# Two transformer blocks on one core: the second block's key search, gated linear attention and attention put in another order

## The reference

```python
proj = h @ w_in                    # q,k,v; q_idx,k_idx,w_idx; gla q,k,v; gdown, ogate
# attention a (8 heads of 64): each query keeps its top-k keys
score = sum_h relu(q_idx . k_idx) * w_idx ; _, sel = top_k(score, 128)
p = softmax(q.k/8 + bias[bucket] over the kept keys) ; o_a = p @ v
# attention b: gated linear attention (4 heads, chunks of 64)
bcum = cumsum(log_sigmoid(gdown @ w_gate_up + b)/16)
q_in, k_in, k_dec = q*exp(bcum), k*exp(-bcum), k*exp(blast - bcum)
o_b = tril(q_in k_in^T) v + q_in state ; state = state*exp(blast) + k_dec^T v
o_b = rmsnorm(o_b) * silu(ogate)
x = x + concat(o_a, o_b) @ w_out ; then a gated FFN and a final norm
```

## Time and profile before

| | us |
|---|---|
| median of 3 runs (lowest, highest) | 2067.23 (2066.11, 2072.78) |
| the profiled execution's own time | 2067.12 |
| its span | 2065.1 |
| PE busy in the span | 1952.7 (95%) |
| DVE, ACT, POOL busy | 889.0, 716.0, 501.8 |

### The profile page before, as it was taken

How to read it: one execution, slowest core, us unless ns; L and a number is a source line. 1 busy time by engine, 2 the same in 40 slices (tenths; PEclk the granted TensorE clock), 3 DMA queues, 4 the chain that set the end, 5 groups by cost and what they waited for, 6 DMA issues and landing times.

```text
span 2065.1 us, 21914 instructions
## 1 busy us (share of the span) xinstructions
PE 1952.7 (95%) x8805; PEld 1523.8 (74%) x8805; DVE 889.0 (43%) x1486; ACT 716.0 (35%) x1032; POOL 501.8 (24%) x272
## 2 busy tenths in 40 slices
PE   7989889999999999999799999998997889999998
PEld 6766667887878777877588888865775678888886
DVE  6677766203041303343233334568435554433443
ACT  5545554232322322433122223423336432222223
POOL 4322224444444434410000000232235401100100
PEclk9999999999999999999899999998999989999999
DMA  9322324521213122325623322421121123232321
GB/s 304 126 82 86 102 78 133 184 87 62 96 62 102 61 82 96 108 82 82 113 82 102 102 86 66 119 62 61 62 69 54 42 72 102 82 102 87 97 92 51
DMA packets 183019, 192.22 MB, mean 93 GB/s; under 512 B 10690, under 2 KB 166632, under 8 KB 182792
## 3 DMA queue, kind: packets, MB, share of 16 engines
q1 hardware_dynamic: 179752, 180.84, 27.4%
q0 software_dynamic: 1744, 4.99, 2.1%
q10 hardware_dynamic: 1424, 5.00, 0.7%
HBM read 186.09 MB, written 4.72 MB: 92 GB/s over the span
## 4 chain that ended last, share of the span: by engine, by line
PE 81%; DVE 12%; DMA 3%; ACT 2%; issue 2%; POOL 0%; SPq 0%; DVEq 0%; ACTq 0%; POOLq 0%
PE bank L1401 21%; PE bank L1402 21%; PE bank L1404 20%; DMA stg<-in_w_ffn_in 2%; PE bank L1421 2%; PE bank L1423 2%; PE bank L1422 2%; PE bank L1506 2%; DVE tmp L1770 1%; DVE spl L1776 1%; DVE SW L2021 1%; DVE sph L1774 1%; DVE small L2019 1%; DVE tmp L1732 1%; PE bank L1462 1%
## 5 line engine op out<-in xcount | busy, mean ns | idle before, releaser
L2543 POOL TENSOR_TENSOR wl<-stg,wh 128x1024 fp32r<-128x1024 f32 x150 | 362.2, 2416 | 973.5 <-ACT wh L2201 973.4
L1401 PE MATMUL bank<-hH,wh 128*128 128x512 f32 x1296 | 543.2, 419 | 22.5 <-DVE wl L1714 14.5
L1402 PE MATMUL bank<-hL,wh 128*128 128x512 f32 x1296 | 521.6, 403 | 0.0
L1404 PE MATMUL bank<-hH,wl 128*128 128x512 f32 x1296 | 520.9, 402 | 0.0
L2201 ACT ACTIVATE wh<-stg 128x1024 fp32r<-128x1024 f32 (+2 forms) x292 | 298.1, 1023 | 327.1 <-PE bank L1404 220.7
L1401 PEld LDWEIGHTS bank<-hH,wh 128*128 128x128 f32 x1296 | 249.4, 192 | 106.5 <-issue 50.7
L1404 PEld LDWEIGHTS bank<-hH,wl 128*128 128x128 f32 x1296 | 249.3, 192 | 61.0
L1402 PEld LDWEIGHTS bank<-hL,wh 128*128 128x128 f32 x1296 | 250.2, 193 | 51.6 <-issue 0.7
L1714 DVE TENSOR_TENSOR wl<-stg,wh 128x1024 fp32r<-128x1024 f32 (+2 forms) x142 | 168.3, 1187 | 252.6 <-ACT wh L2201 252.1
L1401 PE MATMUL bank<-h2H,wh 128*128 128x512 f32 x352 | 141.4, 402 | 0.0
L1402 PE MATMUL bank<-h2L,wh 128*128 128x512 f32 x352 | 140.7, 400 | 0.0
(11 more groups left out here) (323 smaller groups left out, 2760.3 us busy)
## 6 DMA issues: line engine op xcount, KB each, us to landing
stg<-in_w_in SPq DMA_DIRECT2D x54, 1024.0 KB, 5.2
stg<-in_w_ffn_in SPq DMA_DIRECT2D x22, 1024.0 KB, 5.1
stg<-in_w_ada SPq DMA_DIRECT2D x16, 1024.0 KB, 5.3
stg<-in_w_ffn_gate SPq DMA_DIRECT2D x11, 1024.0 KB, 5.3
stg<-in_w_ffn_up SPq DMA_DIRECT2D x11, 1024.0 KB, 5.3
stg<-in_w_ffn_down SPq DMA_DIRECT2D x10, 1024.0 KB, 5.0
stg<-in_w_ada SPq DMA_DIRECT2D x16, 512.0 KB, 6.6
stg<-in_w_proj_ret SPq DMA_DIRECT2D x8, 1024.0 KB, 5.0
```

The source lines that it names most:

```text
L1401: T.matmul(ps, wh, xh, start=j["first"] and k == 0, stop=False)
L1402: T.matmul(ps, wh, xl, start=False, stop=False)
L1404: t = T.matmul(ps, wl, xh, start=False, stop=j["stop"] and last)
L2543: G.tensor_tensor(lo, src, hi, ALU.subtract).then_inc(s["w_lo_pool"], 1)
```

## The change

1. `select` yields twice after each pair of heads. The rate of GQ, GK, GV goes from 0.85 to 0.65.
2. The stage after them holds QA, the four gates, KA (rate 1.1), and VA comes where the gates were (0.97); the first half of w_out goes from 1.0 to 0.97.
3. The gates' products go to `LG` tiles, `gate_silu` follows a job later; `gn` is followed by the product with the gate on POOL.
4. `tm` moves to ACT as a plain copy; the norm is put on after the turn, in four 128-wide activations with `rt3` as scale. The turns take a G bank.
5. `gf`, `gh`, `gi` move from DVE to POOL.
6. `attn` is written anew: bias plus mask (`lg`) one item ahead, `al(n)`, `ae(n-1)`, yield, `at(n-2)`, `lg(n+1)`, `ac(n-2)`, `ag(n)`, yield, `av(n-3)`, `as(n-1)`, yield. `av` takes bank 7, and waits only for its own pair's part of VA.
7. The results of gla have tiles of their own (`goH`, `goL`, where GQ, GK, GV lay) and are split one per job from the attention's start on. `matn` is set at the start of the second block.

```diff
     def turn_after(name, e):
         def turn():
-            take("Z", ("tmt", name, e))
+            take("G", ("tmt", name, e))
...
                 if hh % 2:
                     yield
+                    yield
...
-    stage(0.85)
+    stage(0.65)
...
+                while ("silu", hd) not in p.known:
+                    yield
                 emit("gn", hd)
...
     for e in range(2):
+        fm(2872 + 256 * e, "gate", [(2 * e,), (2 * e + 1,)], after=silu_after)
+    for e in range(2):
         fm(512 + 256 * e, "fm", [("KA", 2 * e), ("KA", 2 * e + 1)])
-    for e in range(2):
-        fm(1024 + 256 * e, "tm", [("VA", 2 * e), ("VA", 2 * e + 1)], after=turn_after)
-    stage(0.9)
+    stage(1.1)
...
         for n in range(len(ITEMS) + 3):
-            for lag, step in ((2, lambda n: emit("as", n)), (1, greatest), (0, logits), (1, lambda n: emit("ae", n)), (3, last),
-                              (2, turned), (2, copied)):
+            if wanted(n, 0):
+                logits(n)
+            if wanted(n, 1):
+                emit("ae", n - 1)
+            yield
+            if wanted(n, 2):
+                turned(n - 2)
+            if n and wanted(n + 1, 0):
+                emit("lg", n + 1)
+            if wanted(n, 2):
+                emit("ac", n - 2)
...
+            if wanted(n, 0):
+                emit("ag", n)
...
+            yield
+            if wanted(n, 3):
+                while ("VA", ITEMS[n - 3][0]) not in p.known:
+                    yield
+                values(n - 3)
+            if wanted(n, 1):
+                emit("as", n - 1)
+            yield
...
     def start_attn():
-        emit("matn")
         p.fore.append(attn())
+        for hd in range(4):
+            p.later.append([hd, lambda hd=hd: split_go(hd)])
...
-    for k0, rate in ((4, 1.0), (0, 0)):
+    for k0, rate in ((4, 0.97), (0, 0)):
...
+            def tm(name, e, n):
+                gb = product(ac, n)
...
+                A_.activation(TMP[2 + e % 2][:, :], gb[:, :], ACTF.Copy).then_inc(empty(("gemm", n, 0)), 1)
...
+                for i in range(4):
+                    t = A_.activation(dst[:, i, :], zb[:, i * P:(i + 1) * P], ACTF.Copy, scale=rt3[:, i:i + 1])
...
+            def gf(r):
+                po.wait_ge("a_ge", r + 1)
+                emptied(po, of_job("fm", "GK", r))
+                G.tensor_tensor(TMP[4][:, :], TMP[4][:, :], GK[:, r, :], ALU.mult).then_inc(s["p_gf"], 1)
```

More of the change, by code:

```diff
@@ L757, in start2 @@
         emit("two_load")
+        emit("matn")
         p.fore.append(factors3())
@@ L776, in turn @@
         def turn():
-            take("Z", ("tmt", name, e))
+            take("G", ("tmt", name, e))
             emit("tmt", name, e)
             give(("tmt", name, e))
+            p.known.add((name, e))
         p.later.append([1, turn])
@@ L891, in make_plan, with silu_after, silu @@
     do(lambda: p.fore.insert(0, interleave(p.fore.pop(0), gla()) if p.fore else gla()))
+    def silu_after(hd):
+        def silu():
+            emit("gate_silu", hd)
+            p.known.add(("silu", hd))
+        p.later.append([1, silu])
     for e in range(2):
@@ L902, in attn, with wanted, logits, turned @@
     def attn():
-        def last(n):
+        def wanted(n, lag):
+            return 0 <= n - lag < len(ITEMS)
+        def logits(n):
+            pr, i = ITEMS[n]
+            if i == 0 and pr + 1 < 4:
+                for hh in range(2):
+                    emit("bias_row", 2 * pr + 2 + hh)
+            for hh in range(2):
+                take("Z", ("al", n, hh))
+            emit("al", n)
+        def turned(n):
+            for hh in range(2):
+                take("C", ("at", n, hh))
+            emit("at", n)
+        def values(n):
             pr, i = ITEMS[n]
             if i == 0:
-                take("G", ("avo", pr), 0)
+                take("O", ("avo", pr), 0)
             emit("av", n)
@@ L915, in last @@
                     pend.append(pr)
[L917 to L939, removed]
         for hh in range(2):
             emit("bias_row", hh)
+        emit("lg", 0)
+        emit("lg", 1)
         for n in range(len(ITEMS) + 3):
-            for lag, step in ((2, lambda n: emit("as", n)), (1, greatest), (0, logits), (1, lambda n: emit("ae", n)), (3, last),
-                              (2, turned), (2, copied)):
[L945 to L948, removed]
+            if wanted(n, 0):
[9 more added lines that the diff above has]
+                emit("ac", n - 2)
+                for hh in range(2):
+                    give(("at", n - 2, hh))
+            if wanted(n, 0):
+                emit("ag", n)
+                for hh in range(2):
+                    give(("al", n, hh))
+            yield
[6 more added lines that the diff above has]
+            yield
@@ L950, in start_attn, with split_go @@
+    def split_go(hd):
+        p.split("h4", 4 + hd, "dve")
+        emit("gos", hd)
     def start_attn():
-        emit("matn")
         p.fore.append(attn())
+        for hd in range(4):
+            p.later.append([hd, lambda hd=hd: split_go(hd)])
     do(start_attn)
     for e in range(2):
-        fm(2872 + 256 * e, "gate", [(2 * e,), (2 * e + 1,)])
-    stage(0.65)
-    def split_go():
+        fm(1024 + 256 * e, "tm", [("VA", 2 * e), ("VA", 2 * e + 1)], after=turn_after)
+    stage(0.97)
@@ L959, in split_go, with h_free @@
+    def h_free():
         p.known.add("h_free")
         p.mark("h4")
-        for hd in range(4):
-            p.split("h4", 4 + hd, "dve")
-            emit("gos", hd)
         for pr in pend:
@@ L966, in split_go @@
             emit("qas", pr)
-    do(split_go)
+    do(h_free)
     def out2_job(f2, k0):
@@ L1080, in program @@
         vw = [(cell(4), cell(4)) for _ in range(2)]
+        rt3 = cell(4)
         with ExitStack() as ph:
@@ L1141, in program @@
             tmp9 = sb("tmp9", [P, S], ctx=ph)
+            with ExitStack() as ph1:
+                GQ = sb("GQ", [P, 2, S], ctx=ph1)
+                GK = sb("GK", [P, 2, S], ctx=ph1)
+                GV = sb("GV", [P, 4, S], ctx=ph1)
+            with ExitStack() as ph1:
+                goH = sb("goH", [P, 4, S], F32R, ctx=ph1)
+                goL = sb("goL", [P, 4, S], F32R, ctx=ph1)
         with ExitStack() as ph:
@@ L1165, in operand @@
                 return orH[:, k, :], orL[:, k, :]
+            if what == "h4" and k >= 4:
+                return goH[:, k - 4, :], goL[:, k - 4, :]
             if what == "mg":
@@ L1652, in av @@
                 pr, i = ITEMS[n]
-                for e in range(4):
-                    emptied(pe, ("tmt", "VA", e))
+                emptied(pe, ("tmt", "VA", pr))
                 emptied(pe, ("at", n, 0))
@@ L1840, in sprd @@
                 ve.wait_ge("v_spread", 5 * i - 4)
+                if key == "n3":
+                    V.tensor_scalar(rt3, w, 1.0, None, ALU.mult).then_inc(s["v_extra"], 1)
                 for c in range(4):
@@ L2075, in gs @@
                 zb = filled(ve, ("gs", hd))
+                ve.wait_ge("p_gh", 2)
                 if hd:
@@ L2453, in gsq, with gate_silu @@
                 A_.activation(tmp8[:, :], TMP[5][:, :], ACTF.Square).then_inc(s["a_gsq"], 1)
[L2455 to L2458, removed]
+            def gate_silu(hd):
+                emptied(ac, of_job("gate", hd))
+                A_.activation(LG[hd][:, :], LG[hd][:, :], ACTF.Silu).then_inc(s["a_gate"], 1)
             def ae(n):
@@ L2601, in al @@
                     po.wait_ge(f"d_bias{bia % 4}", 16 * (bia // 4 + 1))
+                    if n < 2:
+                        po.wait_ge("p_gate", 2 * n + hh + 1)
                     if n >= 3:
@@ L2617, in gpsimd @@
             mine = {"split": split, "n1": n1, "masks": masks_, "sbw": sbw, "ret_load": ret_load, "rot": rot, "rvv": rvv,
-                    "bias": bias, "ffn_a": ffn_a, "gate": gate, "al": al, "qas": qas}
+                    "bias": bias, "ffn_a": ffn_a, "gf": gf, "gh": gh, "gi": gi, "gn": gn, "lg": lg, "qas": qas}
             for name, *at in p.order:
```

80 lines of the change are left out of this document (33 added, 47 removed).

## The result

The changed kernel takes 2035.64 us (median; 2032.27 to 2038.67), the kernel before 2067.88 in the same comparison: ratio 0.9845, 95% interval 0.9829 to 0.9861. Run again later it took 2037.85, ratio 0.9856 (0.9836 to 0.9876). The forecast was 2038.

A forecast was written before the change was run, and what follows sets the result against it. PE's waits, on VectorE's search queue in A and the list's order in B, plus half clock behind them, were taken as the bound. -9.4 and -19.4 make -28.8 on 2067.1: 2038, own range 2024 to 2050, wider 2020 to 2058.

The forecast's parts named there:

- A: Second block, end of MI job to end of VA, 184.0 us before: 18.7 lost in place of 26.9, -9.4 in all.
- B: Attention, from A's end to end of w_out's first half, 112.4 us before: 8 lost in place of 28.6, -19.4.
- 10.7 us of waits: PE's waits left in A: `gt` 3.3, `go` 2.4 and 3.4, another 1 for the rest, 0.6 in tile 3.
- The clock: Half-clock spells of 3.3 us behind PE's waits: two or three in A, 8 us; 3 us in B.
- the search's spread: `select` over 75 turns in place of 63: line 1576's waits (7.3) go but 0.6; DVE nearly full in the next 70 steps.
- the price of `gf` on POOL: POOL's products take 0.1 to 0.64 us longer; only `gf` precedes PE's next step, its cost counted in first `gt`'s 3.3 us.
- rival 3: POOL's six products in gla all stand behind a weight split: 18 us on gla's chain, 2056 us in all; chance 0.05.
- DVE is as good as full, and stalls move rather than vanish: In A's 70 steps after GV, DVE has 66 us of work against PE's 69.
- late hand-overs: In the attention's new loop, engines fit between yields with little to spare; occasional late hand-overs cost 3 us.
- The start: Attention's start: `lg(0)` may wait for bias rows that leave SP only after the weight split two blocks back: 2 us.
- v on ACT: Eight evictions leave DVE, ACT gains about 8.6 us, hidden by its idle time: cost 0, bounds 0 to 2.
- rival 2: B bound by DVE and POOL sharing their access; items stay long, B loses 20, 2051 us in all; chance 0.08.

The follow-up runs named there:

- the second profile: Profile of the changed kernel run again unaltered: A 179.1, B 90.0; median 2037.85 us, ratio 0.9856.
- the first gap: Changed kernel with two more yields between `gf` and the turn `gt`, rate 1.15 for 1.1: 2035.65 us, ratio 0.9848.
- the early bias: Changed kernel with more yields before `gt` and `go`, rate 1.2, plus first item's bias rows and `lg(0)` ahead of gla's last head: 2028.26 us, ratio 0.9803.
- the last version: Changed kernel with more yields before `gt` and `go`, first item's bias and `lg(0)` earlier, and v evicted by VectorE: 2023.96 us, ratio 0.9790.

## Why the prediction came out right, point by point

**The sum.** -9.4 for A and -19.4 for B were forecast, -28.8; measured -6.5 and -23.8, -30.3 (by the second profile -4.9 and -22.4). The total is right because the two errors, 2.9 us too much in A and 4.4 too little in B, have opposite signs; that they nearly cancel is luck. The executions' own spread is as large.

**A: the idle time is right, its places are not.** 10.7 us of waits were forecast; the window has 177.5 - 166.07 = 11.4. The clock kept 0.05 x 177.5 = 8.9, 8 forecast. The prediction put all of A's gain but 1.2 us down to the search's spread; it is needed, but alone it earned nothing. And `gt(0)` was to wait 3.3, `gt(1)` not at all and the two `go` 5.8; they waited 3.0, 4.3 and 2.5. The step that failed is the price of `gf` on POOL ("its price is in the 3.3"): it holds for the first pair only. Its input was misread too: the 1222 ns of VectorE's product "beside POOL's own work" is the mean of one of 0.69 and one of 1.75 us, and only the second met a weight split on POOL (from 1436.08 to 1438.42). DVE's timeline of the kernel before:

```profile
1437.21 1.75 DVE L2043 TENSOR_TENSOR tmp<-tmp,GK 128x512 f32<-128x512 f32 x1
```

The timelines of the changed kernel around the second turn:

```profile
1430.73 0.69 DVE L2058 TENSOR_TENSOR tmp<-tmp 128x512 f32<-128x512 f32 x1
...
1432.18 0.60 ACT L2431 ACTIVATE tmp<-bank 128x512 f32<-128x512 f32 x1 [0.74 <-DVE SW L2029]
1432.67 0.62 ACT L2455 ACTIVATE tmp<-tmp 128x512 f32<-128x512 f32 x1
1433.19 1.05 ACT L2208 ACTIVATE wh<-stg 128x1024 fp32r<-128x1024 f32 x1
...
1434.32 2.34 POOL L2563 TENSOR_TENSOR wl<-stg,wh 128x1024 fp32r<-128x1024 f32 x1 [5.76 <-ACT wh L2208]
1436.62 1.71 POOL L2614 TENSOR_TENSOR tmp<-tmp,GK 128x512 f32<-128x512 f32 x1
...
1438.38 1.11 PE L1466 MATMUL bank<-ident,tmp 128*128 128x128 f32 x4 [4.33 <-POOL tmp L2614]
```

VectorE is done at 1431.4. ACT's exp (2455) stands behind a relu that waits for a score; POOL's product (2614) stands behind a weight split (2563) that itself waits for ACT's high part, which lies behind that exp. Three queues in a row are each passed in their order, and 1.71 us of product end in a wait of 4.3. This is rival 3's mechanism, at one of its six places. On the same k-steps with VectorE's product, in the kernel with the spread alone, `gt` waited 3.6 and at most 0.8, and `go` 5.3: the prediction's waits were those of that kernel. What POOL cost at `gt` came back at `go`, which the prediction had not seen; part of that is how the engines happened to meet (last section).

**Stalls move.** "DVE is as good as full, and stalls move rather than vanish" was half true. DVE isn't full while PE waits for `gt(1)`; windows of 20 us of the changed kernel:

```profile
1400.00:1420.00 20.00, 16.98 (x70) 13.22 (x70) 19.05 (x44) 8.26 (x14) 9.21 (x5) 0.91 0.17 53
1420.00:1440.00 20.00, 14.84 (x56) 9.13 (x57) 13.54 (x15) 9.35 (x16) 8.02 (x5) 0.91 0.17 52
```

In the second PE idles 5.2 us and DVE 6.5. The stall there is latency through three queues. It moved all the same, three times: from `idx2` to `go` with the spread alone, from `gt` to `go` with VectorE's products and with the first gap. A fell clearly further only when both hand-overs were given distance, to 170.2, 171.9 and 167.9; 5.6 of the 9.8 us of waits were still there in the first of these.

**B: too careful.** 8 us were to stay lost; the window has 88.6 - 84.95 = 3.7 idle and clock 1.00 (in the second profile 3.6 and 0.98). The order acts as worked out, but late hand-overs were 2 us, not 3, and they drew almost no half clock. The term that was mis-sized is thus the clock: 3 us forecast, next to none measured. The start was priced right (2; 1.7) for a wrong reason. The changed kernel's timelines of SP and POOL:

```profile
1514.66 0.90 SPq L1361 DMA_DIRECT2D bia<-scratch_bias  x2
...
1524.55 0.86 POOL L2647 TENSOR_TENSOR lg<-bia,matn 128x128 f32<-128x128 f32 x2
```

The bias rows leave SP nine us ahead of `lg(0)`; what holds it is the gate's product and the weight split on POOL, as the early bias shows.

**v on ACT** was priced at 0, with 0 to 2 as bounds. Undone, B is 2.5 to 3.9 us shorter and A the same; undone in the last version, B is 1.4 shorter (88.3 to 86.9) and A 4.0 (171.9 to 167.9). No median tells it apart from nothing, but both point to a loss. The activations with `rt3` as scale:

```profile
L2423 ACT ACTIVATE GV<-bank,small 128x128 f32<-128x128 f32 x16 | 4.6, 378 | 1.2 <-PE bank L1466 1.2
...
1540.11 1.14 ACT L2423 ACTIVATE VA<-bank,small 128x128 f32<-128x128 f32 x4
```

Each took 0.37 to 0.38 us, not 0.27. But they overlap, and four in a row took 1.14 us, close to the 1.08 forecast, so their time is not what the prediction had wrong. The Trainium skill (ScalarE: Activation LUTs, section What ACT_TABLE_LOAD costs) gives about 93 ns for each pointer operand of an activation; the rows nearly agree, 378 against 269 ns. PE did wait for ACT's copies of v, once, 1.1 us; the prediction named that as a sign against it.

**The other signs.** Waits behind `ag` below 4 us: 1.7. Waits left on `gt` with POOL's product and on `go` with the mask product: yes. Clock 0.96 or more in both: B yes, A 0.95. A near 175 and B near 93: 177.5 and 88.6. No table loads among the exps: one is left in B, at its start, where before had nine.

## What to carry to other kernels

A list that several engines walk in order is tuned by the distance between a step that frees a buffer and the step that takes it, and one such distance, between `ag` and the next logits, is the largest part of this gain: alone it brought the ratio to 0.9916 of the whole change's 0.9845, and without it the rest brought 0.9959. When an operation is moved to an emptier engine, look at what stands ahead of it in that engine's queue at that place: here the move shifted the wait by one hand-over. In a chain with several tight hand-overs widen them together and judge by the stretch: the first gap alone showed nothing, both showed 7 to 9 us of A.

## What the runs showed of the hardware

A VectorE operation that meets POOL's weight split can last until the split ends. In the kernel with the products on VectorE, the timelines of DVE and POOL:

```profile
1446.93 2.69 DVE L2029 SCALAR_TENSOR_TENSOR SW<-tmp,WI,SW 128x512 f32<-128x512 f32 x1
1449.68 0.11 DVE L2034 MEMSET SW<- 64x64 f32 x1
1449.83 0.69 DVE L2039 MAX8 small<-SW 128x8 f32<-128x512 f32 x1
...
1446.71 2.35 POOL L2577 TENSOR_TENSOR wl<-stg,wh 128x1024 fp32r<-128x1024 f32 x1 [6.11 <-ACT wh L2222]
```

The score, with two SBUF inputs, took 2.69 us, and ended 0.56 us behind POOL's split. In the changed kernel, where the split began 0.5 us behind it, the same step took 0.74:

```profile
1447.33 0.74 DVE L2029 SCALAR_TENSOR_TENSOR SW<-tmp,WI,SW 128x512 f32<-128x512 f32 x1
...
1448.28 0.69 DVE L2039 MAX8 small<-SW 128x8 f32<-128x512 f32 x1
...
1447.86 2.44 POOL L2563 TENSOR_TENSOR wl<-stg,wh 128x1024 fp32r<-128x1024 f32 x1 [0.46 <-ACT wh L2208]
```

MAX8, with one input, ran inside that split at its 0.69. (The kernel with the spread alone repeats the first case: a split from 1447.59 to 1449.94, a score from 1447.80 that took 2.69.) The Trainium skill (SBUF — State Buffer, section SBUF: two separate sides) says that the two engines share one pair of ports as an exclusive lock, held for a whole instruction, against, among others, VectorE operations with two SBUF inputs; these rows agree.

The score lies in VectorE's queue ahead of the first `go`'s mask product, with nearly no gap between them. That `go` in the kernel with the products on VectorE, then in the changed one:

```profile
1457.38 2.07 PE L1657 MATMUL bank<-tmp,GV 128*128 128x128 f32 x8 [3.77 <-DVE tmp L2099]
...
1455.83 1.16 PE L1657 MATMUL bank<-tmp,GV 128*128 128x128 f32 x8 [0.87 <-DVE tmp L2085]
```

So some 2 us (2.69 - 0.74, an estimate) of the 3.77 are the meeting and not VectorE's products, and the same holds for the 3.8 us of the kernel with the spread alone. The prediction's rival 2 had this as a bound on B, which it isn't: PE is idle there for 3.7 us only.
